# A two-part transformer program on one core: a new opening, moved weight splits, and a shorter end

## What is computed

```
h = h + 0.5 * swiglu(rms_norm(h, ffn1_norm), ffn1_w_in, ffn1_w_out)     # the opening
...
b_gate, c_gate, u = split(h @ w_in, 3);  v = c_gate * u                  # convolution
conv = sum(conv_w[k] * vp[:, k:k + S] for k in range(3))
y = (b_gate * conv) @ w_out
...
x = x + nsa_mixer(h, b_w_qg, b_w_o, shared, rel_bias)                    # sparse block
x = x + squared_relu_mlp(rms_norm(x), mlp_w1, mlp_w2)                    # mlp1
return rms_norm(x, final_norm)                                           # the end
```

## Time and profile before

| | |
|---|---|
| median of 3 runs | 1225.28 us |
| the runs | 1222.89, 1225.28, 1230.53 us |
| profiled execution: time | 1222.8 us |
| profiled execution: span | 1221.0 us |
| TensorE (PE) busy | 1187.0 us, 97% of the span |
| VectorE (DVE) busy | 863.1 us, 71% |
| ScalarE (ACT) busy | 650.4 us, 53% |
| GpSimd (POOL) busy | 216.3 us, 18% |
| DMA | 217.55 MB, mean 178 GB/s |
| mean granted clock of TensorE | 0.995 |

### The profile page before, as it was taken

How to read it: one execution, slowest core, us unless ns; L and a number is a source line. 1 busy time by engine, 2 the same in 40 slices (tenths; PEclk the granted TensorE clock), 3 DMA queues, 4 the chain that set the end, 5 groups by cost and what they waited for, 6 DMA issues and landing times.

```text
span 1221.0 us, 19715 instructions
## 1 busy us (share of the span) xinstructions
PE 1187.0 (97%) x7868; PEld 1062.8 (87%) x7868; DVE 863.1 (71%) x1192; ACT 650.4 (53%) x864; POOL 216.3 (18%) x106
## 2 busy tenths in 40 slices
PE   5999999999999999999999999999998999999996
PEld 4888888988899888888999988888898869888885
DVE  6877667788767887766777776656588775766553
ACT  6555545465655655544643455544356764655431
POOL 1434300000000244410000025510000230454000
PEclk9999999999999999999999999999999999999998
DMA  7555554952345455555435545555576203555540
GB/s 278 207 183 196 202 178 173 283 201 104 104 145 177 171 208 177 203 195 184 173 138 207 204 166 193 196 188 191 191 258 242 105 1 138 207 177 202 179 166 35
DMA packets 31138, 217.55 MB, mean 178 GB/s; under 512 B 3408, under 2 KB 3680, under 8 KB 5584
## 3 DMA queue, kind: packets, MB, share of 16 engines
q1 hardware_dynamic: 29712, 210.85, 48.9%
q0 software_dynamic: 1344, 5.53, 1.6%
HBM read 215.30 MB, written 4.22 MB: 180 GB/s over the span
## 4 chain that ended last, share of the span: by engine, by line
PE 87%; DVE 5%; ACT 4%; issue 3%; DMA 1%; DVEq 0%; ACTq 0%; SPq 0%
PE bank L1415 39%; PE bank L1416 19%; PE bank L1408 7%; PE bank L1409 7%; PE bank L1410 7%; DVE w_hl L743 1%; ACT w_hl L395 1%; PE bank L1491 1%; PE bank L1492 1%; PE bank L1493 1%; DVE hid_f L1179 1%; PE bank L1767 1%; PE bank L1669 1%; PE bank L1499 0%; PE bank L1657 0%
## 5 line engine op out<-in xcount | busy, mean ns | idle before, releaser
L743 DVE TENSOR_TENSOR w_hl<-raw,w_hl 128x2048 fp32r<-128x2048 f32 x196 | 448.4, 2289 | 119.8 <-ACT w_hl L395 118.8
L395 ACT ACTIVATE w_hl<-raw 128x2048 fp32r<-128x2048 f32 x197 | 373.9, 1901 | 120.0 <-PE bank L1410 54.3
L1415 PE MATMUL bank<-x_hl,w_hl 128*128 128x512 f32 x864 | 302.8, 396 | 12.6 <-DVE w_hl L942 12.6
L1415 PE MATMUL bank<-hidden,w_hl 128*128 128x512 f32 x864 | 299.7, 394 | 0.0
L351 POOL TENSOR_TENSOR hidden<-hid_f,hidden 128x256 fp32r<-128x256 f32 (+1 forms) x76 | 189.4, 2492 | 531.3 <-ACT hidden L479 313.5
L1416 PE MATMUL bank<-x_hl,w_hl 128*128 128x256 f32 x864 | 240.5, 278 | 0.0
L1416 PE MATMUL bank<-hidden,w_hl 128*128 128x256 f32 x864 | 239.3, 277 | 0.0
L1415 PEld LDWEIGHTS bank<-x_hl,w_hl 128*128 128x128 f32 x864 | 163.1, 189 | 50.5 <-issue 12.6
L1415 PEld LDWEIGHTS bank<-hidden,w_hl 128*128 128x128 f32 x864 | 162.0, 188 | 37.6
L1408 PE MATMUL bank<-x_hl,w_hl 128*128 128x256 f32 x576 | 164.6, 286 | 1.5 <-DVE w_hl L743 1.5
L458 ACT ACTIVATE second<-bank 128x512 f32<-128x512 f32 (+1 forms) x108 | 57.6, 533 | 199.3 <-PE bank L1416 199.3
(11 more groups left out here) (337 smaller groups left out, 1536.1 us busy)
## 6 DMA issues: line engine op xcount, KB each, us to landing
raw<-weights SPq DMA_DIRECT2D x198, 1024.0 KB, 4.8
bias_skew<-bias_rows POOLq DMA_DIRECT2D x1, 3072.0 KB, 27.4
gate_or_bias<-bias_skew POOLq DMA_DIRECT2D x1, 2048.0 KB, 10.6
h<-x_t SPq DMA_DIRECT2D x1, 1024.0 KB, 4.9
out_t<-x_f SPq DMA_DIRECT2D x4, 256.0 KB, 2.3
con<-consts SPq DMA_DIRECT2D x1, 769.5 KB, 12.5
heads<-p_t POOLq DMA_DIRECT2D x1, 256.0 KB, 2.9
par<-small SPq DMA_DIRECT2D x1, 200.0 KB, 5.0
```

Of the source, the lines that this page charges most:

```text
L395: nc.scalar.activation(dst, src, ACT.Copy).then_inc(hi_split, 1)
L743: V.tensor_tensor(w_lo[:, s, :], raw[:, s, :], w_hi[:, s, :].bitcast(F32), ALU.subtract).then_inc(lo_split, 1)
L1415: mm(out_, w_hi[:, s, c:c + m], x, start=start, stop=False, **kw)
```

## The change

Eight edits, in the program's order.

1. SyncE loads x in two halves, the 8 columns of ffn1 gains by themselves (128 x 8), chunk 0 in two halves, and the rest of the parameters behind chunk 2. ScalarE loads its Ln/Exp table before any data has come, and ScalarE and VectorE work by halves: 4 tiles of the operand, 2 quarters of chunk 0, twice; then chunk 1 in two halves.
2. TensorE runs 25 matmuls on a tile of zeros (512 columns each, bfloat16) before its first real one. It takes chunk 1 in halves, and sums the squares after chunk 1, no longer after chunk 0. VectorE splits chunk 2 after its sums, and adds up the product of tile 0 and splits chunk 3 before the Newton step.
3. Convolution: VectorE and ScalarE split chunk conv_in+3 before the factor's Ln/Exp and Newton step, no longer in turn 0. Turn 0 is written out, turns 1 to 3 stay a loop.
4. The first two chunks of conv_out are multiplied together: pieces 0 to 2 of both, then piece 3 of both (`two_pairs`, as before for other stages).
5. Sparse block, first half: VectorE splits nsa_q2 before query(1) and the lo part of blk_v; nsa_q3 is split in halves, before `phi_silu(0)`; the split after the last phi chunk, `nxt(PHI[3])`, goes behind the first scores; ScalarE's `phi_gate` is cut into the copy and the sigmoid.
6. Sparse block, loop: ScalarE splits nsa_out+2 in turn 8, VectorE splits nsa_out+1 and +2 behind the loop. VectorE makes the operand pieces of nsa_out (`merged`) later in its list, and TensorE multiplies pieces of nsa_out chunk 0 in turns 8 and 9, then chunks 0 and 1 by pieces, into other banks of PSUM.
7. End: the last tile of the last down-projection uses `product` (three 256-column matmuls) so that no half has to be copied and added; the sum of squares is split, tiles 0 to 6 early and tile 7 by itself, with 4 matmuls on zeros between; ScalarE multiplies h by the final gain tile by tile (`gained_out`), and VectorE multiplies twice as wide at the end (4 instructions for 8).
8. Five of ScalarE's table loads go.

```diff
 @block.sync
-            sp.dma_start(h[:, :, :], x_t).then_inc(x_in, 16)
-            sp.dma_start(par[:, :], small).then_inc(small_in, 16)
-            for c in range(RING):
+            sp.dma_start(h[:, 0:4, :], x_t[:, 0:4, :]).then_inc(x_in[0], 16)
+            sp.dma_start(par[:, 0:KT], small[:, 0:KT]).then_inc(gain_in, 16)
+            sp.dma_start(raw[:, 0, 0:CH // 2], weights[0, :, 0:CH // 2]).then_inc(first_in, 16)
+            sp.dma_start(h[:, 4:8, :], x_t[:, 4:8, :]).then_inc(x_in[1], 16)
+            sp.dma_start(raw[:, 0, CH // 2:CH], weights[0, :, CH // 2:CH]).then_inc(raw_landed[0], 16)
+            for c in range(1, RING):
                 sp.dma_start(raw[:, c, :], weights[c]).then_inc(raw_landed[c], 16)
+            sp.dma_start(par[:, KT:N_SMALL], small[:, KT:N_SMALL]).then_inc(small_in, 16)
...
 @block.tensor
             pe.wait_ge(setup, 4)
+            for n in range(WARM):
+                mm(bank[:, SUMS, :], zeros[:, 0:P], zeros[:, :], start=True, stop=True)
             feed_forward("ffn1", x_hl, 1)
...
-                    if j == 0:
+                    if j == (1 if stage == "ffn1" else 0):
                         sum_squares(norm_no)
...
-            project("conv_out", range(4), y_hl, "conv")
+            c = C["conv_out"]
+            two_pairs(c, (0, 1), y_hl, "conv", 3)
+            for j in range(2, 4):
+                arrived(c + j + 1)
+                pair((c + j) % RING, j, y_hl).then_inc(chunk_used, 1)
...
+                if t == PAIRS:
+                    pe.wait_ge(n_max, 2 * PAIRS)
+                    out_piece(0, 0)
...
+                if t == PAIRS + 1:
+                    out_piece(0, 1)
...
-            pe.wait_ge(op_lo, PC["o_nsa"] + 3)
-            project("nsa_out", range(4), y_hl, "o_nsa")
+            out_piece(0, 2)
+            for p in range(3):
+                out_piece(1, p)
+            for j in range(2):
+                out_piece(j, 3)
...
-            sum_squares(11)
+            pe.wait_ge(sum_ready, 11)
+            mm(bank[:, SUMS, 0:S], ones[:, :], sq[:, 0, :], start=True, stop=False)
+            for n in range(4):
+                mm(bank[:, 4, :], zeros[:, 0:P], zeros[:, :], start=True, stop=True)
+            pe.wait_ge(sq_ready, SQ["final"] + KT)
+            mm(bank[:, SUMS, 0:S], ones[:, :], sq[:, KT - 1, :], start=False, stop=True).then_inc(ss_ready, 1)
...
 @block.vector
-            factor("mix0")
+            c0 = C["conv_in"]
+            mean_square("mix0", bank[:, SUMS, 0:S])
+            nxt(c0)
+            newton("mix0", r_sb[:, :])
...
             factor("final")
-            for t in range(KT):
-                ins = V.scalar_tensor_tensor(out=x_f[:, t, :], in0=h[:, t, :], scalar=col("final", t),
-                                             in1=r_sb[:, :], op0=ALU.mult, op1=ALU.mult)
+            dve.wait_ge(gained, KT)
+            for j in range(UPDATES):
+                y = out_g[:, 2 * j:2 * j + 2, :]
+                V.tensor_tensor(y, y, r_two, ALU.mult).then_inc(y_ready, 1)
```

More of the change, by code:

```diff
@@ L40 @@
 SKEW = LINE + 1
+WARM = 25
 UPDATES = 4
@@ L502, in downs @@
                         nc.scalar.activation(sq[:, o, :], h[:, o, :], ACT.Square).then_inc(sq_ready, 1)
+                        if following == "final" and o < KT - 1:
+                            gained_out(o)
                     if used and o == KT - 1:
                         nxt(c)
[L505 to L513 removed]
@@ L516, in _ @@
+            act.wait_ge(raw_landed[1], 16)
+            for q in range(2):
+                a = slice(1024 * q, 1024 * q + 1024)
+                nc.scalar.activation(w_hi[:, 1, a], raw[:, 1, a], ACT.Copy).then_inc(first_hi if q < 1 else hi_split, 1)
             for j in range(4):
                 square(j)
-            rsqrt("ffn1")
+            split(2, 2, 1)
+            s = 2 * SLOTS[0]
+            act.wait_ge(chunk_used, 1)
+            second_half("ffn1", 0, second[:, 0, :, :], bank[:, s:s + 2, S:2 * S])
@@ L519, in _ @@
+            nxt(0)
+            rsqrt("ffn1", load=False)
+            nc.scalar.preload_act_table_set("sigmoid_and_others")
             ups("ffn1")
+            act.wait_ge(small_in, 16)
             downs("ffn1", "mix", x_h)
@@ L1479, in up, with up_halves @@
                 return last
+            def up_halves(slot, x):
+                for half in range(2):
+                    if half == 0:
+                        pe.wait_ge(first_lo, 4)
+                    else:
+                        arrived(2)
+                    for t in range(2):
+                        for k in range(KT // 2 * half, KT // 2 * (half + 1)):
+                            last = wide(bank[:, 2 * slot + t, :], 1, k * 256 + t * P, P, x[:, k, :, :], k == 0,
+                                        k == KT - 1)
+                return last
             def tokens(s, bk, width, kts, x, base, first, last_):
```

264 lines of the change are left out of this document (178 added, 86 removed).

## The result

The changed kernel takes 1211.91 us (median of 4 runs, 1208.83 to 1213.55), the kernel before 1224.9 in the same comparison: a ratio of 0.9899 with a 95% interval of 0.988 to 0.9918. It is 13.0 us, or 1.0%, faster; forecast were 1213 and 11.2. The profiled execution is the fastest of the four (1208.83, span 1207.0, 1.8 around it).

The account below looks back on a forecast made before the run. TensorE, busy 1187.0 of 1221.0 us, was taken as the bound, leaving 34.0 idle. Gains 4.0 + 1.2 + 2.8 + 1.7 + 1.5 = 11.2 us gave 1211.6 or 1214.1 by footing; 1213 was taken, range 1207.5 to 1218.

Parts of the forecast that it names:

- Opening, 4.0 forecast: Start to ffn1: chunk 4's split ends at 34.8, TensorE came there at 38.8 before; gain 4.0, bounds -0.5 and 5.2.
- the wait before chunk 4: Opening, ffn1: TensorE finishes chunks 2 and 3 at 32.5 and waits 2.3 us for VectorE's split, ending at 34.8.
- at 421 GB/s the 0.7 MB that go from ahead of it are worth 1.7 us: Opening's loads: half of x lands at about 4.6 and the gains with it (5.0).
- Convolution, 1.2 forecast: Convolution: of the 1.5 wait for conv_in+3, 0.3 is kept; conv_out's remaining 0.8 go whole, 0.8 to 1.0; together 1.2.
- the second split of the turn is where it was: Convolution, VectorE: second split stays at 631.68 to 634.0, the third at 638.10 to 640.4; TensorE waits 0.6 for each.
- rival D: More than forecast: half-rate stretch around 957 falls away (1.5), or written-out turn 0 is shorter on VectorE (1.2); 1210.3; chance 0.15.
- Sparse block, 4.5 forecast: Sparse block: first half gains 2.8 (bounds 0.5 and 3.4) from moved splits, the loop 1.7 (bounds 0 and 1.9).
- End, 1.5 forecast: After mlp1: copy and adding go, last multiplications about 2.9; gain 1.4, with 0.1 for TensorE's second, shorter sum; bounds 0.8 and 2.0.
- B: Opening brings nothing: zeros don't raise the clock or end late; -0.5 for 4.0, total 1217.5; chance 0.11.
- C: Loads set the times in the sparse block's first half, so 2.3 of the 2.8 don't come; 1215.3; chance 0.08.
- F: Moved splits wait for ScalarE in their new places; only end and conv_out remain, 2.5; 1221; chance 0.02.
- E: Slower: a lower granted clock in the feed-forward blocks, every 1% costing 11.9 us; 1237 at 0.975; chance 0.02.

Follow-up runs that it names:

- e5: The changed kernel with the split of conv_in+3 back in the convolution's turn 0, which stays written out; 1213.71 us.
- e6: The changed kernel with conv_out multiplied in its old order and the four matmuls on zeros at the end left out; 1213.4 us.
- e1: The changed kernel without its 25 matmuls on zeros at the start; 1214.49 us.
- e2: The changed kernel with x and chunk 0 each loaded in one piece instead of two halves; 1210.68 us.
- e9: The changed kernel with x and chunk 0 loaded whole and the sparse block's 32 narrow products spread between wider matmuls; 1207.9 us.
- e10: The kernel of e9 without the 25 matmuls on zeros at the start; 1211.06 us.
- e3: The kernel before with the 25 matmuls on zeros at the start and nothing else; 1225.68 us, 1.001 of before.
- e4: The kernel before with 9 matmuls on zeros filling the gap ahead of the sparse block's phi products; 1223.27 us, 0.9994 of before.
- e7: The changed kernel with VectorE's splits of nsa_q2 and the last phi chunk back at their old places in the sparse block; 1218.3 us.

## Why the prediction was right, and where it was off

The total and the bound were right, since each wait was read at its place. Opening and end came out within half a us of their terms; convolution and sparse block gained more than theirs, by 1.2 and 2.1 in the profiles. That the median came within 1.1 us of the forecast is in part luck. The four runs lie at 1208.8, 1210.3 and twice at 1213.5; the steps of 1.5 and 4.7 are the size of the dip and of the dip with the slower rate of ffn1 (1.45 and 3.3, last section), which no term had, and the median falls between them.

**Opening, 4.0 forecast, 3.55 in the profiles.** Zeros to 10.0 (10.19), a warm start and the wait before chunk 4 on VectorE's split (35.35 for 34.8) are right. Wrong is the step "at 421 GB/s the 0.7 MB that go from ahead of it are worth 1.7 us": a rate read from transfers in one piece was taken for others. The first half of chunk 0 was ready at 9.02, not 6.9, and the sum came at 22.57 for 21.4. In e5 and e6, whose first half came at 7.2, the sum came at 21.51 and 21.33, so this step fails in four profiles of six and not in all. The wait before chunk 4 was 0.88 for 2.3, since TensorE came there 2.0 later than forecast: 1.2 by the late sum, and 0.8 because chunks 2 and 3 took 11.9 us from the sum for the 11.1 reckoned, in e6 too. VectorE's split came only 0.55 later. That the term came out nearly right is owed to this last step, which was reckoned on VectorE's chain; and the zeros, to which I gave 2.1 of TensorE's time, are worth half a us in this kernel (e1) and 1.7 where the data come in time (e2, e9, e10).

**Convolution, 1.2 forecast, 2.44.** The failed step is "the second split of the turn is where it was": turn 0 written out has shorter pauses between VectorE's dependent operations than the loop (0.04 for 0.15 to 0.2, in turns 0 and 1 of the same trace), and its splits came 0.96 and 1.26 nearer. Neither wait of 0.6 came. That is the second half of rival D; that the term is off by just the 1.2 that I had priced there is chance, since most of it is conv_out's. And the terms are not independent: conv_out's order was worth 1.83, not 0.8 to 1.0 (e6), because a TensorE that no longer waits in the turn waits longer at the next place.

**Sparse block, 4.5 forecast, 6.56.** First half and loop are right in place and releaser: no wait at nsa_q2, 0.70 at nsa_q3 (0.5 forecast), none before the phi products and none late in the loop. Of the 2.1 above the forecast, 1.45 is the dip of the clock that this execution did not have, the first half of rival D; e3 and e4 show that the old order lacks it at times too, so it belongs to the two profiles and not to the change. Against 145.8 without dip the block gained 5.1. TensorE's waits in it add up to 6.33 before and 1.65 after, 4.7 less, so about 0.4 have no wait to show for them.

**End, 1.5 forecast, 1.45.** From the last matmul of mlp1 to the end 10.4 us, as forecast. The end's zeros are worth nothing (e6), as the sum had them. The terms as I listed them add up to 1.4, so the 1.5 had 0.1 that no term carries. The last multiplications took 2.49, not the 2.9 reckoned, so some other part gave 0.4 less than its term. No run takes the other parts of the end, or the five table loads, one by one: their share is argued from the marks alone.

Without the dip the profiles give 3.55 + 2.44 + 5.1 + 1.45 = 12.5 us; the medians differ by 13.0. Of the rivals, B is half true (the zeros bring little here, but the order does), C and F fall with e7, E never showed, and both halves of D came.

## What to carry to other kernels

A wait that is removed can come back at the next place unless that is opened too (0.80 at conv_out became 1.55): price the edits of one stage as a chain, not one by one. Before transfers are cut up to start sooner, measure when the pieces land; here the whole loads beat the halves by 1.0 to 2.2 us. Where thin matmuls stand together or behind a wait, look for the clock at half behind them; spreading them won 1.5 us here. And put a warm-up only where no long wait lies between it and the work: over 2.13 us of idle time it held, within 3.43 it was lost (e3).
